# Decode NSA: phi_w1 products ahead of the values, values set aside by GpSimd, three turn banks; dilated decode attention: selection rounds spread over the batch

## The reference, cut to what matters

```
# layer 0, mixer A: each of the 64 decode tokens keeps 256 of the 2056 keys by an indexer's score
_, idx = lax.top_k(score, 256)
# layer 0, mixer B (dilated): softmax(q k + bias) v over the held positions, 8 heads
logits = einsum('bqhe,bqkhe->bqhk', q, kg) * SCALE;  p = softmax(logits + bias);  o = einsum('bqhk,bqkhe->bqhe', p, vg)
# layer 1, mixer C (NSA): compressed, selected and window branches, mixed by gates
ha = einsum('bcjge,jef->bcgf', ch, w1[:16]);  hb = einsum('bcjge,jef->bcgf', ch, w1[16:])   # phi_w1 products
h = gelu(ha[:, :-1] + hb[:, 1:] + const);  kc = einsum('bcgf,fe->bcge', h, w2)              # for keys and for values
imp = softmax(q kc).sum(heads);  chosen = top_k(block sums of imp + bonus, 16)
o = g0 * o_cmp + g1 * softmax(q k_slc + bias, chosen blocks) v_slc + g2 * softmax(q k_win + bias) v_win
```

## Time and profile before

| what | before |
|---|---|
| runs, median (lowest to highest) | 2809.2 us (2801.62 to 2817.05), 3 runs |
| the profiled execution | 2816.06 us, its span 2814.3 us |
| dilated decode attention (sb_) | from about 371.6 to 613.3 us of the span |
| decode NSA (sc_) | from about 1879 to 2226 us |

### The profile page before, as it was taken

One profiled execution on the slowest core, in us unless ns is written; L12 is line 12 of the kernel. 1 busy time (PEld: TensorE's weight loads), 2 busy tenths in 40 slices (PEclk: granted clock), 3 DMA queues, 4 the chain that ended last, 5 costly groups with the idle time before them and its releaser, 6 DMA issues. The chain is left out here.

```text
span 2814.3 us, 41116 instructions
## 1 busy us (share of the span) xinstructions
PE 2243.7 (80%) x15442; PEld 1833.4 (65%) x15442; DVE 1336.9 (48%) x2667; ACT 910.1 (32%) x1497; POOL 140.7 (5%) x405
## 2 busy tenths in 40 slices
PE   5895755547767789998977777967888778999896
PEld 1895323325535689997867775545666568999784
DVE  2222437874656435554452215853444544555444
ACT  0210222211236235453331104752333313454332
POOL 0001000000000111110010000000000011111001
PEclk9997767768889889999988857987999888999998
DMA  2455166513132065564204232124333206656321
GB/s 62 139 189 176 25 207 225 188 49 144 66 120 93 9 195 200 194 212 139 79 8 134 91 50 68 54 82 116 128 136 136 75 6 196 209 191 222 119 76 41
DMA packets 166928, 341.04 MB, mean 121 GB/s; under 512 B 37726, under 2 KB 104334, under 8 KB 162810
## 3 DMA queue, kind: packets, MB, share of 16 engines
q1 hardware_dynamic: 151584, 200.99, 23.0%
q10 hardware_dynamic: 11756, 83.75, 8.6%
q0 software_dynamic: 3456, 54.53, 5.0%
HBM read 312.33 MB, written 97.35 MB: 146 GB/s over the span
## 5 line engine op out<-in xcount | busy, mean ns | idle before, releaser
L216 PE MATMUL ffn_acc<-x_h,ffn_wh 128*128 128x288 f32 x1408 | 303.8, 297 | 6.0 <-DVE ffn_wl L208 6.0
L216 PE MATMUL ffn_acc<-x_l,ffn_wh 128*128 128x288 f32 x1408 | 302.9, 297 | 0.0
L216 PE MATMUL ffn_acc<-x_h,ffn_wl 128*128 128x288 f32 x1408 | 302.9, 297 | 0.0
L216 PEld LDWEIGHTS ffn_acc<-x_h,ffn_wh 128*128 128x128 f32 x1408 | 228.8, 190 | 6.2 <-issue 6.2
L216 PEld LDWEIGHTS ffn_acc<-x_l,ffn_wh 128*128 128x128 f32 x1408 | 228.7, 190 | 0.0
L216 PEld LDWEIGHTS ffn_acc<-x_h,ffn_wl 128*128 128x128 f32 x1408 | 228.5, 190 | 0.0
L1720 PE MATMUL ffn_acc<-ffn_wh,x_h 128*128 128x512 f32 x440 | 175.4, 399 | 22.1 <-DVE ffn_wl L208 22.1
L208 DVE TENSOR_TENSOR ffn_wl<-ffn_w,ffn_wh 128x2048 fp32r<-128x2048 f32 (+1 forms) x88 | 154.3, 1755 | 69.8 <-ACT ffn_wh L1748 69.8
L1721 PE MATMUL ffn_acc<-ffn_wl,x_h 128*128 128x512 f32 x440 | 173.2, 394 | 0.0
L1722 PE MATMUL ffn_acc<-ffn_wh,x_l 128*128 128x512 f32 x440 | 173.1, 393 | 0.0
L208 DVE TENSOR_TENSOR x_l<-ffn_hid,x_h 128x1152 fp32r<-128x1152 f32 x44 | 59.8, 1358 | 165.1 <-ACT x_h L1806 165.1
(11 more groups left out here) (409 smaller groups left out, 4744.7 us busy)
## 6 DMA issues: line engine op xcount, KB each, us to landing
out_s_b_kv<-state_b_kv ACTq DMA_DIRECT2D x80, 768.0 KB, 7.8
ffn_w<-ffn_up SPq DMA_DIRECT2D x44, 1024.0 KB, 10.5
ffn_w<-ffn_down SPq DMA_DIRECT2D x44, 512.0 KB, 3.7
sb_k<-state_b_kv SPq DMA_DIRECT2D x8, 2048.0 KB, 11.5
sb_v<-state_b_kv SPq DMA_DIRECT2D x8, 2048.0 KB
proj_ab_w<-w_in_ab SPq DMA_DIRECT2D x11, 1024.0 KB, 5.3
proj_c_w<-w_in_c SPq DMA_DIRECT2D x7, 1024.0 KB, 5.5
hT_ab<-proj_ab_stage ACTq DMA_DIRECT2D x22, 288.0 KB, 2.1
```

What stands on the lines that cost most here:

```text
L216: done = pe.matmul(o, weights, x, start=start, stop=stop)
```

## The change

In the dilated attention the rounds of a batch stand in other places: none at the head, two behind the shift (batch 0 too), one between the probability copies and `o`, and one behind `o`; `mix_in(b)` stands behind that last round instead of behind the next shift.

In NSA the tps banks are three and hps is gone: the phi_w1 products go to two of the three logit banks and wait for the shifts that read these banks last (dots 4 and 5 of the batch before). GpSimd copies a batch's values out of kv into a tile v of their own (128x2048); `values` reads v and waits for the copy (v_ready); the next gather into the slot waits for that copy and for the batch's turns. hidden(a=1) stands ahead of the p turns and `values`, with a k group behind each of its four groups. The x groups stand one place earlier between the dots; the pw turns stand ahead of importance, dots 2 behind the window values. ACT does the k copies ahead of Gelu. DVE's additions of hidden wait for all eight groups and stand between its copies of p groups 0, 1 and 2. xT has 6 slots in place of 8; q lies in the tile shifted.

```diff
-        def select(dve, b, part):
-
-            each = selection.ROUNDS // (2 * NB)
-            for r in range(each):
-                selection.round(dve, (2 * b + part) * each + r)
+        def select(dve, b, first, rounds):
+
+            each = selection.ROUNDS // NB
+            for r in range(first, first + rounds):
+                selection.round(dve, b * each + r)
...
         def _(dve):
-            select(dve, 0, 0)
...
-                if b:
-                    mix_in(b - 1)
-                    select(dve, b, 0)
+                select(dve, b, 0, 2)
...
-                select(dve, b, 1)
+                select(dve, b, 2, 1)
...
+                select(dve, b, 3, 1)
+                mix_in(b)
 
...
-        tps = [p.ps(f"tps{i}", [P, 512]) for i in range(2)]
-        hps = p.ps("hps", [P, 512])
+        tps = [p.ps(f"tps{i}", [P, 512]) for i in range(3)]
-        h_bank = (hps[:, 0:256], outp[:, 256:512])
...
         for b in range(-1, NB):
             if b + 1 < NB:
-                turns += [("x", b + 1, i) for i in range(8)]
+                turns += [("x", b + 1, i) for i in range(8)] + [("k", b + 1, i) for i in range(4)]
             if b >= 0:
                 turns += [("p", b, i) for i in range(5)]
             if b + 1 < NB:
-                turns += [("k", b + 1, i) for i in range(4)] + [("kw", b + 1, 0), ("pc", b + 1, 0)]
+                turns += [("kw", b + 1, 0)]
             if b >= 0:
                 turns += [("pw", b, i) for i in range(2)]
+            if b + 1 < NB:
+                turns += [("pc", b + 1, 0)]
...
+        def h_bank(c, g):
+
+            return logit[(7 * c + g) % 3]
...
-                if b >= 2:
-                    pool.wait_ge(slc_out, b - 1)
...
+            gather(0)
+            pool.wait_ge(tabled, 4)
+            gather(1)
+            for c in range(NB):
+                pool.wait_ge(kv_in[c % 2], 16 * (c // 2 + 1))
+                if c:
+                    pool.wait_ge(slc_out, c)
+                pool.tensor_copy(v[:, :, :], kv[:, c % 2, :].rearrange("p (j n) -> p j n", j=STRIDE)[:, :, 384:512]).then_inc(v_ready, 1)
+                if c + 2 < NB:
+                    pool.wait_ge(v_ready, c + 1)
+                    n = turn_no[("k", c, 3)]
+                    for m in range(n - 2, n + 1):
+                        pool.wait_ge(tps_turned[m % 3], m // 3 + 1)
+                    gather(c + 2)
...
-                    else:
-                        pe.wait_ge(h_summed, 4 * c)
+                    for n in (7 * c - 3, 7 * c - 2) if c else ():
+                        pe.wait_ge(shifted_out[n % 3], n // 3 + 1)
...
+                last.then_inc(h_done, 1)
...
+                if i == 0:
+                    pe.wait_ge(v_ready, b + 1)
...
-                            probs, value = pT[:, j, r], kv[:, b % 2, j * 512 + 384 + r.start:j * 512 + 384 + r.stop]
+                            probs, value = pT[:, j, r], v[:, j, r]
...
+                if c < NB:
+                    turn_x(c, 0)
+                if b >= 0:
                     dots(b, 3)
                     pick(b, 3)
                 if c < NB:
-                    turn_x(c, 0)
                     turn_x(c, 1)
                 if b >= 0:
                     dots(b, 4)
                     pick(b, 4)
+                if c < NB:
+                    turn_x(c, 2)
+                if b >= 0:
                     dots(b, 5)
                 if c < NB:
-                    turn_x(c, 2)
                     turn_x(c, 3)
                 if b >= 0:
                     dots(b, 6)
...
                     for f in range(4):
                         hidden(c, 0, f)
                         turn_x(c, 4 + f)
+                    for f in range(4):
+                        hidden(c, 1, f)
+                        turn_k(c, f)
                 if b >= 0:
                     turn_p(b, 0)
                     for i in range(5):
...
                             turn_p(b, i + 1)
                         values(b, i)
                 if c < NB:
-                    for f in range(4):
-                        hidden(c, 1, f)
-                    for i in range(4):
-                        turn_k(c, i)
                     turn_kw(c)
                     compressed(c)
                     dots(c, 0)
                     cmp_scores(c)
                     dots(c, 1)
-                    dots(c, 2)
+                if b >= 0:
+                    turn_pw(b)
+                if c < NB:
                     importance(c)
                 if b >= 0:
-                    turn_pw(b)
                     window_values(b)
+                if c < NB:
+                    dots(c, 2)
...
+                    for i in range(4):
+                        turned(("k", c, i), kT[:, i * 512:(i + 1) * 512])
+                    act.copy(kT[:, PAST:LS], k_new[:, 0, c * NS:(c + 1) * NS]).then_inc(kT_new, 1)
                     for a in range(2):
                         act.wait_ge(h_summed, 4 * c + 2 * a + 2)
                         act.activation(hid[:, a, :, :], hid[:, a, :, :], ACT.Gelu_apprx_tanh, bias=keep.cmp_const[:, a:a + 1]).then_inc(activated, 1)
-                    for i in range(4):
-                        turned(("k", c, i), kT[:, i * 512:(i + 1) * 512])
-                    act.copy(kT[:, PAST:LS], k_new[:, 0, c * NS:(c + 1) * NS]).then_inc(kT_new, 1)
...
-                    if c:
-                        act.wait_ge(cmp_out, c)
-                    turned(("pc", c, 0), pcT[:, :], NC, P)
                 if b >= 0:
                     if b:
                         act.wait_ge(win_out, b)
                     for i in range(2):
                         copy_probs(act, act.copy, pwT, ("pw", b, i))
+                if c < NB:
+                    if c:
+                        act.wait_ge(cmp_out, c)
+                    turned(("pc", c, 0), pcT[:, :], NC, P)
...
-                if b >= 0:
-                    for i in range(5):
+                for i in range(5):
+                    if b >= 0:
                         copy_probs(dve, dve.tensor_copy, pT, ("p", b, i))
-                if c < NB:
-                    for a in range(2):
-                        hidden(c, a)
+                    if c < NB and i < 2:
+                        hidden(c, i)
```

More of the change, by code:

```diff
@@ L2185, in _, with gather @@
         def _(pool):
-            for b in range(NB):
-                if b == 1:
-                    pool.wait_ge(tabled, 4)
-                if b >= 2:
-                    pool.wait_ge(slc_out, b - 1)
-                pool.indirect_dma_start(out=kv[:, b % 2, :], out_offset=None, in_=rows_in_cache,
-                                        in_offset=bass.IndirectOffsetOnAxis(ap=keep.chunk_row[:, b:b + 1], axis=0)).then_inc(kv_in[b % 2], 16)
+            def gather(c):
+                pool.indirect_dma_start(out=kv[:, c % 2, :], out_offset=None, in_=rows_in_cache,
+                                        in_offset=bass.IndirectOffsetOnAxis(ap=keep.chunk_row[:, c:c + 1], axis=0)).then_inc(kv_in[c % 2], 16)
+            gather(0)
[12 more added lines that the diff above has]
+                    gather(c + 2)
         @block.sync
@@ L2218, in turn @@
                 n = turn_no[group]
-                if n >= 2:
-                    pe.wait_ge(tps_out[n % 2], n // 2)
+                if n >= 3:
+                    pe.wait_ge(tps_out[n % 3], n // 3)
                 for i, src in enumerate(sources):
-                    last = pe.transpose(tps[n % 2][0:rows, i * P:(i + 1) * P], src, keep.ident[:, :])
-                last.then_inc(tps_turned[n % 2], 1)
+                    last = pe.transpose(tps[n % 3][0:rows, i * P:(i + 1) * P], src, keep.ident[:, :])
+                last.then_inc(tps_turned[n % 3], 1)
             def turn_x(c, i):
@@ L2241, in hidden @@
                         r = slice(g * HD, (g + 1) * HD)
-                        last = pe.matmul(h_bank[g][:, a * P:(a + 1) * P], w1[r, a, j, :], xT[r, a, j, :], start=(j == 0), stop=(j == STRIDE - 1))
-                if f == 3:
-                    last.then_inc(h_done, 1)
+                        last = pe.matmul(h_bank(c, g)[:, a * P:(a + 1) * P], w1[r, a, j, :], xT[r, (4 * a + f) % 6, j % 4, :], start=(j == 0), stop=(j == STRIDE - 1))
+                last.then_inc(h_done, 1)
             def compressed(c):
@@ L2431, in turned @@
                 n = turn_no[group]
-                act.wait_ge(tps_turned[n % 2], n // 2 + 1)
-                act.copy(dst, tps[n % 2][0:rows, 0:width]).then_inc(tps_out[n % 2], 1)
+                act.wait_ge(tps_turned[n % 3], n // 3 + 1)
+                act.copy(dst, tps[n % 3][0:rows, 0:width]).then_inc(tps_out[n % 3], 1)
             sample_table(act, nat, vec, KIND_FULL, 0, N_HEADS, 0, LS, loaded)
@@ L2513, in hidden @@
             def hidden(c, a):
-                dve.wait_ge(h_done, 2 * c + 2)
+                dve.wait_ge(h_done, 8 * c + 8)
                 if c:
```

35 lines of the change are left out of this document (18 added, 17 removed).

## The result

The changed kernel took 2745.36 us, the median of four runs from 2744.68 to 2745.53; the kernel before, on the same chip, 2812.03, from 2801.62 to 2817.05. It lies inside the wide range of 2738 to 2790, but outside the forecast's own 2750 to 2775 and next to the 2747 of the rival in which the clock stays up.

What follows compares the result with a forecast made beforehand. DVE was taken to pace the dilated attention and PE to pace NSA. From 2816.1 us, gains of 29.4 (dilated attention), 16.4 (NSA iterations) and 3.4 (head) gave 2766.9; with the median 6.9 lower, 2760, range 2750 to 2775.

Steps and rivals of the forecast that it cites:

- the rival in which the clock stays up: NSA, behind pick: the granted clock does not fall, 4.2 us gained an iteration instead of 2.3; 2747 us, chance 0.22.
- The ring: Dilated attention: PE's scores wait for `o`, DVE's next shift waits for the scores; a period falls from 26.41 to 22.3 us.
- The half microsecond of waiting: Dilated attention: DVE waits for PE's scores and turn of `o` ahead of `mix_in`, about half a us a batch.
- the rival of the keys: Dilated attention: ACT's copies of the next batch's keys become the bound, turns move out by 4.65; 2789 us, chance 0.05.
- The forecast's own case: NSA: the clock falls behind pick as now, 2.3 us gained an iteration; 2760 us, range 2750 to 2775, chance 0.50.
- pick to products: NSA, from pick to the phi_w1 products, 9.27 us before: 1.3 gained an iteration, bounds 0.5 and 3.7.
- second half with kw: NSA, second half of the products with k groups, plus kw: 7.18 us for what took 8.97, 1.79 gained.
- p turns and values: NSA: DVE's additions between its p copies make this part 6.5 us instead of 5.78, 0.75 lost.
- the chain from compressed products to pick: NSA, compressed softmax and choice, where PE, DVE and ACT answer one another: unchanged, 0 counted.
- where the clock falls elsewhere: NSA: the clock falls over p turns and values instead, an iteration 1.5 us longer than now; 2787 us, chance 0.16.
- The 3.4: NSA head: k copies ahead of Gelu let batch 0's compressed products start 3.4 us earlier, bounds 0 and 3.4.
- The rule of the Trainium skill: A GpSimd operation started first holds DVE operations with two SBUF inputs or two-port modes throughout; an 8.8 us copy costs about 20.

Runs made afterwards that it cites:

- the fills undone: Changed kernel with dots 2 back ahead of the pw turns and the x groups back behind dots 3 and 4: 2768.3 us.
- no copy: Changed kernel without GpSimd's copy: values read from the gathered slot, and the gather of batch c + 2 waits until the values of batch c are out: 2800.8 us.
- the first experiment: Kernel before with only the dilated attention of the changed kernel, NSA left as before: 2783.9 us, ratio 0.9896.
- the long copy: Changed kernel with GpSimd's copy of the values done as an addition of a tile of zeros: 2752.7 us.

## Why the prediction was right, and where its sizes were off

*Dilated attention.* The ring and its terms held: 22.07 for 22.3. The half microsecond of waiting was put at the wrong place, ahead of `mix_in`. PE's scores and turn of `o` ended in time (467.49 + 0.40 against 468.00), and `mix_in` took 0.40 in the ring, while PE's turns of the probabilities came 0.4 to 0.8 late: they stand behind the next batch's key turns, which wait for ACT's copies (3.19 in the batch shown), so the rival of the keys holds on a small scale. Moving `mix_in` into that wait took 0.36 a batch off. The prediction counted 0.35 gained by taking `mix_in` from behind the shift; but in those five batches the copies come 11.2 to 11.65 behind the shift without it, and they came 11.30 behind it with it, so it was all but free there.

*NSA.* The forecast's own case, a clock that falls behind pick as before, did not come; its rival did. The mis-sized term is pick to products, 1.3 between bounds of 0.5 and 3.7. It measured 9.27 - 5.95 = 3.32: the clock stayed up, the rival with a chance of 0.22, whose 4.2 an iteration is near the 4.8 that six of seven gained. The others were near: second half with kw 13.33 - 6.61 + 0.59 = 7.31 for 7.18, with the first half put at the 6.61 of before; p turns and values 6.35 for 6.5; the chain from compressed products to pick 0.4 shorter where 0 was counted. "...whether this is enough I can't read from rows" is where the forecast stopped. What the runs show: with a wait of 2.09 us put back, and nothing else changed, the clock fell in every iteration although the fills stood; with the fills undone and no such wait, it fell behind some picks only. Over all traces, the clock falls once in each later iteration where PE waits 2 us or more in it (the kernel before, the dilated attention alone, the wait put back, no copy), and in none of the seven that have the new order without such a wait. So for the changed kernel the wait is shown to be enough. That the wait for k copies brought the fall about in the kernel before is the reading that fits: in the first experiment the same code has it right behind that wait. It is not shown, as no run takes this wait alone from the kernel before, and there the fall stands 9.7 us behind the wait's end.

How near the rival's 2747 came is in part luck. The profiled executions differ by 22 us more than the 49.2 forecast; 10.0 of these lie outside both phases, 2.2 behind the last choice, and 9.3 in the iterations, where the first lost 5.3 on its forecast and the others gained 14.6. And one sum of the rivals doesn't come out: where the clock falls elsewhere, 3 lost against the 1.79 - 0.75 = 1.04 gained is 1.96 an iteration, not 1.5, and 2790 in place of 2787.

*Head and first iteration.* The 3.4 came (2.9), and the mishap named against it too: x 0 waits 2.00 for the gather. The first interval is no measure of the change: with the NSA of before it was 41.54 in the first experiment and 35.72 in the kernel before itself.

*GpSimd's copy.* 1.89 where 2.5 was taken, near the memset's 1.81. The rule of the Trainium skill (SBUF — State Buffer, section "SBUF: two separate sides") was left open by the earlier trace rows; the long copy agrees with it, if DVE's scaling from SBUF to SBUF is one of the two-port operations, which no row shows. It shows the size, too: one operation was held, and only until GpSimd ended. At 1.89 no operation of DVE in that chain grew longer. The rows next to the earlier trace rows, in the trace of before, could have told as much, for operations with two inputs in SBUF:

```profile
2266.70 1.23 DVE L1350 TENSOR_TENSOR xtok<-xtok,out_c_g 128x1024 f32<-128x1024 f32 x1 [0.89 <-ACT xtok L1363]
2267.95 0.82 DVE L1352 TENSOR_TENSOR xtok<-xtok,out_c_b 128x640 f32<-128x640 f32 x1
2268.70 2.04 DVE L1350 TENSOR_TENSOR xtok<-xtok,out_c_g 128x1024 f32<-128x1024 f32 x1
```

```profile
2268.00 1.66 POOL L1370 TENSOR_TENSOR xtok<-xtok,out_c_b 128x384 f32<-128x384 f32 x1 [112.68 <-DVE xtok L1350]
```

DVE's multiplication of 1024 values, both operands in SBUF, takes 1.23 by itself and 2.04 where it begins under GpSimd's addition, which ends at 2269.66. So the price of a held operation stood in the trace of before.

## What to carry to other kernels

A short wait of the matrix engine beside small products can cost twice, once as a wait and once by the clock behind it (2.09 us became 4.8): look at windows of the granted clock before a wait is called cheap, and count both prices. Look at more than one execution before a fall of the clock is tied to a place: the same code had it at two. Where an engine carries independent rounds for another phase, put them where the trace shows it waiting for something else, at the head and in the first batch above all, and move small copies into the wait that is left. A copy that frees a buffer early is paid for by the transfer that it lets start: here 1.89 us of GpSimd for some 8 us of the period, 6.2 of them waiting.

## What the runs showed of the hardware that was not expected

GpSimd's addition of 2048 values took 4.51 us, 2.2 ns a value; the forecast's 4.3 came from 384 values in 1.66. In the rows above, that addition begins 0.05 behind DVE's, which ends at 2268.77; from there to its own end, 2269.66, it is 0.89, or 2.3 ns a value. So it seems to have been held in its turn, and about half of the 1.66 to be waiting. This is an estimate: no run takes the neighbour away.

The period with the wait put back, 37.63 falling to 37.55, is that of the first experiment to 0.02 in every later iteration, and that of the kernel before (37.54 to 37.58) nearly so, although the waits stand at different places and so do the falls of the clock; why stays open.
